# The opening of a two-block transformer program: fewer modulation blocks ahead of the first GEMM, the first norm's statistics earlier, the first gate at its use

## The reference

```
ml = (silu(c)     @ w_mod[i] + b_mod[i])        # 9 vectors of 1024: (shift, scale, gate) x 3
mc = (silu(c_ctx) @ w_mod[i] + b_mod[i])        # the same weights, for the 256 context tokens
ada_in(h, g, m, j)       = rms_norm(h, g) * (1 + m[j, scale]) + m[j, shift]
gated_residual(h,m,j,y,w) = h + w * m[j, gate] * y
h  = gated_residual(h,  ml, 0, swiglu(ada_in(h,  norm_g[i,0], ml, 0), w_in, w_out), 0.5)
hc = gated_residual(hc, mc, 0, swiglu(ada_in(hc, norm_g[i,0], mc, 0), w_in, w_out), 0.5)
... a mixer (retention in layer 0, neighbourhood attention in layer 1), a second FFN; then the second model
```

## Time and profile before

| | |
|---|---|
| time, median of 3 runs (lowest, highest) | 3647.98 us (3647.9, 3655.38) |
| span of the profiled execution | 3645.0 us |
| TensorE busy | 91% |
| VectorE, ScalarE, GpSimd busy | 55%, 32%, 21% |
| loads | 421 MB, 116 GB/s |

### The profile page before, as it was taken

The page is one execution under the profiler, slowest core; times in us unless marked ns, Lnnn a source line. Parts: engine busy times, 40 slices in busy tenths (PEclk is TensorE's granted clock), DMA queues, the critical chain, the costliest instruction groups (busy, mean ns, idle before and its releaser), DMA issues. The chain is left out here.

```text
span 3645.0 us, 47063 instructions
## 1 busy us (share of the span) xinstructions
PE 3299.3 (91%) x18721; PEld 2761.1 (76%) x18721; DVE 2000.6 (55%) x3354; ACT 1173.3 (32%) x1965; POOL 783.2 (21%) x974
## 2 busy tenths in 40 slices
PE   7999989999799898899989999988787998788898
PEld 3788868888577676588867778987576997668798
DVE  1677663454488788533343345554555665454666
ACT  2322233222331121322232334443344343333443
POOL 3578720000169999200000000000000000000000
PEclk9999999999999899899999999999899998899899
DMA  7445431221244554423232224652133553223353
GB/s 229 116 149 169 132 130 54 81 87 58 64 116 148 156 154 141 120 75 112 79 97 64 61 58 133 189 171 80 47 116 127 162 180 99 69 86 105 126 181 105
DMA packets 501219, 421.37 MB, mean 116 GB/s; under 512 B 9946, under 2 KB 497674, under 8 KB 501000
## 3 DMA queue, kind: packets, MB, share of 16 engines
q1 hardware_dynamic: 497976, 412.33, 36.8%
q0 software_dynamic: 3024, 6.03, 0.7%
HBM read 417.20 MB, written 1.12 MB: 115 GB/s over the span
## 5 line engine op out<-in xcount | busy, mean ns | idle before, releaser
L1111 DVE TENSOR_TENSOR w_low<-raw,w_high 128x1024 fp32r<-128x1024 f32 (+2 forms) x720 | 807.0, 1162 | 404.0 <-ACT w_high L786 403.0
L786 ACT ACTIVATE w_high<-raw 128x1024 fp32r<-128x1024 f32 (+2 forms) x720 | 648.2, 948 | 848.3 <-PE gemm L1614 502.4
L1614 PE MATMUL gemm<-xh,w_high 128*128 128x512 f32 (+1 forms) x1792 | 682.6, 381 | 56.3 <-DVE xl L1139 55.3
L1614 PE MATMUL gemm<-xl,w_high 128*128 128x512 f32 (+1 forms) x1792 | 670.4, 374 | 0.0
L1614 PE MATMUL gemm<-xh,w_low 128*128 128x512 f32 (+1 forms) x1792 | 669.8, 374 | 0.0
L1614 PEld LDWEIGHTS gemm<-xh,w_high 128*128 128x128 f32 x1792 | 343.0, 191 | 140.5 <-issue 49.5
L1614 PE MATMUL gemm<-yh,w_high 128*128 128x256 f32 (+1 forms) x1344 | 391.2, 291 | 22.4 <-DVE yl L1139 16.6
L1614 PEld LDWEIGHTS gemm<-xh,w_low 128*128 128x128 f32 x1792 | 343.8, 192 | 64.2
L1614 PEld LDWEIGHTS gemm<-xl,w_high 128*128 128x128 f32 x1792 | 344.3, 192 | 60.9 <-issue 0.7
L1614 PE MATMUL gemm<-yl,w_high 128*128 128x256 f32 (+1 forms) x1344 | 383.0, 285 | 0.0
L1614 PE MATMUL gemm<-yh,w_low 128*128 128x256 f32 (+1 forms) x1344 | 382.3, 284 | 0.0
(11 more groups left out here) (290 smaller groups left out, 4967.3 us busy)
## 6 DMA issues: line engine op xcount, KB each, us to landing
raw<-in_ffn_w_in SPq DMA_DIRECT2D x176, 512.0 KB, 5.2
raw<-in_w_mod SPq DMA_DIRECT2D x72, 1024.0 KB, 6.5
raw<-in_w_in SPq DMA_DIRECT2D x50, 1024.0 KB, 5.2
raw<-in_w_up SPq DMA_DIRECT2D x32, 1024.0 KB, 5.5
raw<-in_w_down SPq DMA_DIRECT2D x32, 1024.0 KB, 5.2
raw<-in_ffn_w_out SPq DMA_DIRECT2D x32, 768.0 KB, 4.7
raw<-in_ret_w_in SPq DMA_DIRECT2D x24, 1024.0 KB, 5.2
raw<-in_ffn_w_out SPq DMA_DIRECT2D x32, 640.0 KB, 4.2
```

The source lines that it names most:

```text
L786: act.activation(wh[i % SPL][:, a:b], raw[slot_of["w", i]][:, a:b], ACT.Copy).then_inc(w_high, 1)
L1111: dve.tensor_tensor(wl[i % SPL][:, a:b], raw[slot_of["w", i]][:, a:b], wh[i % SPL][:, a:b].bitcast(F32), ALU.subtract).then_inc(w_low, 1)
L1614: ins = pe.matmul(out, l_, r_, start=first and j == 0, stop=last and j == 2)
```

## The change

MOD0 goes from 12 to 8: blocks 8 to 11, the first gate, leave TensorE's opening and are woven into the first FFN with the others, so 28 blocks stand there where 24 stood, at floor(9 i / 7). The first norm's squares and square root move on ScalarE ahead of the tiny activations, its eight matmuls on TensorE behind mod_rows of block 4, its reciprocal on VectorE behind the lambdas. coefficients is cut in two: the scales are made in the opening and raise a new semaphore, for which GpSimd waits; the gate is made between the first input and the first output GEMM, where VectorE waits for the four blocks to have been taken. TensorE's wait for coef_ready goes.

```diff
-MOD0 = 12
+MOD0 = 8
...
+        first_scales = sem("first_scales_ready")
...                                             # GpSimd
-            pool.wait_ge(coef_ready, 1)
+            pool.wait_ge(first_scales, 1)
...                                             # ScalarE
-            def norm(name):
+            def mean_square(name):
...
+            def norm(name):
+                N = norms[name]
+                X_h, X_l, x_t, s_q = N["buf"]
+                tok = N["tok"]
+                if name != "n00":
+                    mean_square(name)
                 if N["how"] == "split":
...
                 act.activation(h[:, c, :], aux[c % 4][:, :], ACT.Copy).then_inc(h_init, 1)
+            mean_square("n00")
             act.wait_ge(small_in, 80)
...                                             # VectorE
+            def inverse_root(name):
...
+                if name != "n00":
+                    inverse_root(name)
                 dve.wait_ge(rstd_ready, u + 1)
...
-            def coefficients(i):
+            def scales(i):
...
+            def gates(i):
+
+                m0 = NMOD * (i // 3) + 24 * (i % 3)
                 dve.tensor_scalar(half[:, i, :, :], mod[:, m0 + 16:m0 + 24, :], 1.0 if i % 3 == 1 else 0.5, None,
                                   ALU.mult).then_inc(coef_ready, 1)
...
+            inverse_root("n00")
             for q in range(1, MOD0 // 4):
                 take_rows(q)
             dve.wait_ge(mod_out, MOD0 // 4)
...
-            coefficients(0)
+            scales(0)
+            dve.sem_inc(first_scales, 1)
 
             def ffn(l, f, j):
                 norm(f"n{l}{j}")
                 for s in range(2):
                     run(gemm(f"in{l}{f}{s}"))
+                    if (l, f, s) == (0, 0, 0):
+                        while len(taken) < 12 - MOD0:
+                            take_mod(MOD0 + len(taken))
+                        dve.wait_ge(mod_taken, 12 - MOD0)
+                        gates(0)
+                        dve.wait_ge(coef_ready, 1)
                     run(gemm(f"out{l}{f}{s}"))
...                                             # TensorE
             for b in range(4, MOD0):
                 mod_rows(b)
+                if b == 4:
+                    norm("n00")
                 if b > 4:
                     mod_turn(b - 1)
             mod_turn(MOD0 - 1)
             pe.wait_ge(mod_row, MOD0)
 
             def ffn(l, f, j):
-                norm(f"n{l}{j}")
+                if (l, j) != (0, 0):
+                    norm(f"n{l}{j}")
...
-            pe.wait_ge(coef_ready, 1)
             ffn(0, 0, 0)
```

More of the change, by code:

```diff
@@ L787, in splits_upto @@
                     split[0] += 1
-            def norm(name):
+            def mean_square(name):
                 N = norms[name]
-                X_h, X_l, x_t, s_q = N["buf"]
+                s_q = N["buf"][3]
                 u, tok = N["u"], N["tok"]
@@ L1122, in norm @@
                 dve.reciprocal(rstd[:, 0:tok], std[:, 0:tok]).then_inc(rstd_ready, 1)
+            def norm(name):
+                N = norms[name]
+                X_h, X_l, x_t, s_q = N["buf"]
+                u, tok = N["u"], N["tok"]
+                if name != "n00":
+                    inverse_root(name)
                 dve.wait_ge(rstd_ready, u + 1)
@@ L1325, in coefficients @@
                                                    op0=ALU.add, op1=ALU.mult))
+            def gates(i):
+                m0 = NMOD * (i // 3) + 24 * (i % 3)
                 dve.tensor_scalar(half[:, i, :, :], mod[:, m0 + 16:m0 + 24, :], 1.0 if i % 3 == 1 else 0.5, None,
                                   ALU.mult).then_inc(coef_ready, 1)
+            def coefficients(i):
+                scales(i)
+                gates(i)
             dve.wait_ge(vec_turned, 3)
```

## The result

The changed kernel takes 3666.88 us in the median of its runs (3658.59 to 3668.43), beside 3648.94 for the kernel before on the same chip: 1.0041 times the time, 95% interval 1.0028 to 1.0053. Slower, and 2.2 us from the forecast of 3664.7. The profiled spans are 3664.4 and 3645.0, 19.4 us apart, where the sum said 16.7.

The account below looks back on a forecast made before the run. TensorE, busy 91% of the span, was taken as the bound, with GpSimd's pace setting the price in the first FFN's output GEMMs. -4.5 (opening) + 3.2 (adds) + 18.0 (waits) = +16.7 on 3648.0: 3664.7 us, range 3641 to 3680.

Parts of the forecast that it names:

- Parts 2 and 3: Opening: moved statistics delay ScalarE's steps, scales only 1.3 us early; xt and xl slowed beside GpSimd, 4.5 us gained.
- The hole: Opening: TensorE waits 4.6 us for ScalarE's delayed copy of row 4, ahead of the turn of block 4.
- Part 4, the pace: First FFN's output GEMMs: GpSimd takes 13.1 us a woven block, five continuous blocks ending 91.5 us from w9 or w27.
- Part 4, the sum: First FFN: GpSimd's late blocks cost TensorE 18.0 us of waits, all in the two output GEMMs.
- my 82.2: First output GEMM: us from w9's start at which unhindered TensorE wants the last of the continuous woven blocks.
- rival (c): Worse: GpSimd stalls also drop the clock and VectorE becomes a third queue, 10 to 15 us more, 3677; chance 0.12.
- the upper bound of the price: Output GEMMs: with 14 us a GpSimd block the loss is 26 us.
- (a): Output GEMMs: GpSimd keeps up, falling towards 11.3 us a block; +0.7 us in all, 3649; chance 0.14.
- the 13.1: First FFN: GpSimd's us per woven block, read over six blocks from 234.90 to 315.70 us before the change.
- (b): Faster: the opening pays in full, -20.5 us, -12 in all with Part 4 at 3.2 + 5, 3636; chance 0.11.
- the 1.62: First norm: us from piece to piece of xt and xl while GpSimd works, against 0.79 when it is idle.
- nothing changes: Behind the first FFN: the later 36 blocks stand where they stood, in the same slots, so no time changes.

Follow-up runs that it names:

- Act_order: The changed kernel with the first norm's statistics behind mod_rows of block 6 and its squares behind ScalarE's copy of row 5; 3658.94 us, 1.0036 of the kernel before.
- late_gpsimd: The changed kernel with GpSimd starting its first woven block only when all 16 xl of the first norm are made; 3653.05 us, 1.0004 of the kernel before.
- half_gpsimd: The changed kernel with GpSimd making half the columns in seven of eight products and seven sums per woven block, results incomplete; 3561.16 us, 0.9762 of the kernel before.
- late_act12: The changed kernel with twelve blocks kept in the opening, plus the edits of act_order and late_gpsimd; 3635.48 us, 0.9969 of the kernel before.
- all_three: The changed kernel with act_order, late_gpsimd and the 28 woven blocks placed more sparsely in the output GEMMs; 3634.41 us, 0.9959 of the kernel before.

## Why the prediction was right, step by step

**The opening, Parts 2 and 3: right.** The hole is 4.42 (4.6), the last turn ends at 68.83 (69.0 with the 2.5 for the clock), block 6 takes 6.06 for 16 matmuls where they took 3.6, so 2.5 at half. First xt 75.93 (76.2), last xl 99.77 (100.5), first add -4.2 (-4.5). Act_order and late_gpsimd show both causes by taking them away.

**Part 4, the pace: right.** I had the last block of the first output GEMM ready 91.5 behind w9's start, which is 204.25 here; the add at 294.54 is 90.3 behind. w19 was to be ready at 101.5 and began at 101.1. In the second output GEMM it was 91.5 behind w27 (402.85), and the add came 91.2 behind. Five blocks at 13.1 are five at 13.1.

**Part 4, the sum: right; what it is made of: partly wrong, and the match to the decimal is luck.** The price is 18.0, as predicted, and half_gpsimd, which makes it vanish, shows that all of it hangs on GpSimd's work, with what that does to VectorE. But I wrote of it as waits of about 18 us with "matmul time unchanged". Waits are 10.7 more, and 6.8 is the clock. How the two combine is seen beside half_gpsimd, which has the same adds in the same places, from add to add:

| stretch | the change | half_gpsimd | difference |
|---|---|---|---|
| add ahead of w9 to the last block's add | 203.44 to 294.54 | 195.43 to 279.74 | 6.8 |
| to the add ahead of w27 | to 402.04 | to 382.89 | 4.4 |
| to the last woven block's add | to 494.02 | to 469.21 | 5.7 |
| to the next norm | to 514.89 | to 488.44 | 1.6 |

The first and the third are GpSimd's lateness. Two of the four slow stretches lie in them (284 to 288, 458 to 463) and cost nothing of their own: TensorE still waits at the add that ends each (0.57 and 1.76), and at full clock would have waited that much longer. The second is w19's wait of 2.6 and the 1.7 of the slow stretch behind it, the fourth the 1.6 of the slow stretch behind the last add: there TensorE is late for nothing, and the clock is on top. So lateness is 15.1 (6.8, 2.6, 5.7) where I had 18.0 (9.3, 2.2, 6.5), mostly because the unhindered TensorE is slower to the first of these adds than my 82.2 (83.5 by half_gpsimd) and GpSimd a little faster than my 91.5 (90.3); and 3.3 of clock, a small part of rival (c), makes up for it. The waits also stand mostly at w_low (9.1), not at the adds (2.3): a late block frees its slot late, and VectorE, behind its sums, splits the next weights late. I had allowed that for w19 only.

**Two slips that changed nothing.** Before the change ten pieces of the norm ran without GpSimd, not eleven; and with 14 us a block the upper bound of the price is 27 by the same sum, not 26.

**The rivals.** (a), that GpSimd keeps up, falls by the 13.1. (b), that the opening pays in full, falls by the hole and the 1.62; but late_act12 and all_three show that it was only some changes of order away: 10.8 and 26.3 us at the first add. (c)'s clock drops came, with 3.3 us on top and not 10 to 15.

**Left open.** From the next norm to the end the change is 2.4 us longer with the same work of TensorE. The nine kernels that have that work spread over 8.8 us there, and nothing was tried on it. That the whole came out within 2.2 us of the forecast is finer than this spread, and so in part luck too.

## What to carry to other kernels

A step that fills one engine's hole is also put into the queues of the others: follow every instruction of it on each engine, in order, and ask who stands behind it (here ScalarE's squares ahead of eight tiny activations and a copy). An engine at 21% of the span can still be the bound of one stage; compare its pace per block with the consumer's there, and when it is close, spread the blocks, or give a share to an engine that has room, as ScalarE had here. Measure the two halves of a change apart, since here the one undid the other.

## What the runs showed that I had not expected

- VectorE and GpSimd slow each other both ways. Halving GpSimd's work took 41.6 us off VectorE's untouched multiply-adds (743 to 531 ns), halving the columns of those took 16 us off GpSimd's untouched work.
- TensorE's clock fell behind short stops. From 282 to 284 TensorE was busy 1.03 of 2 us, and from 284.5 to 287.9 it ran at half; from 303 to 305 not busy at all, at half from 305 to 308.4; from 456 to 458 1.00 of 2, at half from 458.6 to 462; from 492 to 494 0.27 of 2, at half from 496.1 to 499.5. But a wait of 1.49 us at 247.46 left it at full, as did 0.68 at 257.63 and 0.57 at 274.71: the length of a single stop doesn't tell here which of them the clock will follow. Each fall took 1.7 us of TensorE's work, of which two (behind 305 and 496) showed in the time.
- The second FFN, a window of 150 us, in the kernel before:

```profile
1100.00:1250.00 150.00, 129.52 (x542) 103.22 (x541) 116.96 (x157) 24.27 (x32) 143.65 (x176) 0.90 0.45 140
```

And in half_gpsimd, which has the same matmuls to do and gets through more of them in this window:

```profile
1100.00:1250.00 150.00, 149.34 (x697) 122.54 (x697) 112.94 (x190) 33.63 (x43) 130.76 (x221) 1.00 0.62 187
```

GpSimd is busy 143.7 of 150, TensorE 129.5 at 0.90 of its clock: the kernel before was bound by GpSimd there. With half of GpSimd's work, and VectorE the faster for it, half_gpsimd runs the whole from the next norm on in 3073.9 us for 3147.1. I had read this stretch as "nothing changes", which was true, and passed by 40.7 us of TensorE's waits.
